# One level of Strassen's algorithm in the input projection of a fused decoder block

## The reference, cut to what matters

```
u = rms_norm(h, attn_pre_norm)                       # 1024 x 1024
c_q, c_kv, k_rope, m_q, m_k, m_v, m_o, m_i, m_f = split_cols(u @ w_in, IN_SIZES)
# widths       256   128   64      512  512  512  512  4    4
q  = rms_norm(c_q, q_norm) @ w_uq;   kv = rms_norm(c_kv, kv_norm) @ w_ukv
qk = silu(causal_dwconv(concat([m_q, m_k]), conv_w, conv_b))     # four taps along the sequence
hm = rms_norm(mlstm_chunkwise(mq, mk, m_v, m_i + bias_i, m_f + bias_f))
mlstm_out = sigmoid(m_o) * hm
```

## Time and profile before

| | |
|---|---|
| median of 3 runs | 1843.81 us |
| the profiled execution, from its first to its last instruction (span) | 1841.5 us |
| median less that span | 2.3 us |
| TensorE busy | 1815.9 us, 99% of the span |
| VectorE, ScalarE, GpSimd busy | 74%, 35%, 58% |

### The profile page before, as it was taken

The page is one execution under the profiler, slowest core; times in us unless marked ns, Lnnn a source line. Parts: engine busy times, 40 slices in busy tenths (PEclk is TensorE's granted clock), DMA queues, the critical chain, the costliest instruction groups (busy, mean ns, idle before and its releaser), DMA issues.

```text
span 1841.5 us, 22556 instructions
## 1 busy us (share of the span) xinstructions
PE 1815.9 (99%) x8610; PEld 1517.1 (82%) x8610; DVE 1360.6 (74%) x1530; ACT 640.1 (35%) x1140; POOL 1065.2 (58%) x749
## 2 busy tenths in 40 slices
PE   8999999999999999999999999999999999999998
PEld 8887889988887888888878888788788888888887
DVE  7777146666587666586589989667988885698897
ACT  5421157772331111111133433515433343333313
POOL 4443332260149988798877885632575455566564
PEclk9999999999999999999999999999999999999999
DMA  6121210033222333233366641112333232853232
GB/s 168 48 57 46 51 23 17 17 91 116 91 81 69 107 100 122 73 115 114 115 244 210 221 149 47 46 44 94 106 123 115 103 111 106 319 191 107 73 111 91
DMA packets 123322, 194.81 MB, mean 106 GB/s; under 512 B 31169, under 2 KB 87489, under 8 KB 120146
## 3 DMA queue, kind: packets, MB, share of 16 engines
q1 hardware_dynamic: 123184, 193.34, 31.2%
q10 hardware_dynamic: 34, 0.07, 0.0%
HBM read 144.56 MB, written 48.82 MB: 105 GB/s over the span
## 4 chain that ended last, share of the span: by engine, by line
PE 68%; DVE 5%; issue 2%; POOL 2%; ACT 1%; DMA 0%; DVEq 0%; SPq 0%; POOLq 0%
PE ps L1211 61%; PE ps L1517 1%; PE ps L1519 1%; PE ps L1518 1%; POOL ring_lo L1082 1%; POOL ring_hi L1081 1%; DVE y L3165 1%; PE ps L1764 1%; PE ps L1766 1%; PE ps L1765 1%; DVE y L3158 0%; PE ps L1642 0%; DVE xs_lo L2992 0%; DVE y L2883 0%; PE ps L1396 0%
## 5 line engine op out<-in xcount | busy, mean ns | idle before, releaser
L1211 PE MATMUL ps<-f_hi,ring_hi 128*128 128x512 f32 x384 | 149.7, 390 | 1.3 <-POOL ring_lo L1082 1.3
L1211 PE MATMUL ps<-f_hi,ring_lo 128*128 128x512 f32 x384 | 149.4, 389 | 0.0
L1211 PE MATMUL ps<-f_lo,ring_hi 128*128 128x512 f32 x384 | 149.4, 389 | 0.0
L972 POOL TENSOR_TENSOR w_lo<-stage,w_hi 128x1024 fp32r<-128x1024 f32 x48 | 125.7, 2618 | 4.0
L1145 POOL TENSOR_TENSOR ring_lo<-w_sum,ring_hi 128x512 fp32r<-128x512 f32 x60 | 95.3, 1600 | 50.2 <-ACT ring_hi L2215 50.1
L1211 PE MATMUL ps<-d_w_hi,d_hid_hi 128*128 128x512 f32 x312 | 121.5, 390 | 1.5 <-DVE hid L2858 1.1
L1082 POOL TENSOR_TENSOR ring_lo<-w_sum,ring_hi 128x512 fp32r<-128x512 f32 x80 | 118.4, 1480 | 6.7
L1211 PE MATMUL ps<-d_w_lo,d_hid_hi 128*128 128x512 f32 x312 | 121.4, 389 | 0.0
L1211 PE MATMUL ps<-d_w_hi,d_hid_lo 128*128 128x512 f32 x312 | 121.4, 389 | 0.0
L2115 ACT ACTIVATE f_copy<-ps 128x512 f32<-128x512 f32 x60 | 35.4, 597 | 226.2 <-PE ps L1211 207.3
L971 POOL TENSOR_SCALAR w_hi<-stage 128x1024 fp32r<-128x1024 f32 x48 | 61.5, 1281 | 73.6 <-PE ps L1211 61.5
(11 more groups left out here) (484 smaller groups left out, 5533.9 us busy)
## 6 DMA issues: line engine op xcount, KB each, us to landing
d_raw<-hid_rows SPq DMA_DIRECT2D x37, 512.0 KB, 4.5
stage<-in_w_up SPq DMA_DIRECT2D x22, 512.0 KB, 4.8
wd_raw<-in_w_down SPq DMA_DIRECT2D x22, 512.0 KB, 5.3
raw_w<-in_w_gate SPq DMA_DIRECT2D x20, 512.0 KB, 4.8
stage<-in_w_in SPq DMA_DIRECT2D x18, 512.0 KB, 3.7
stage<-in_pool_w_in SPq DMA_DIRECT2D x16, 512.0 KB, 5.1
raw_w<-in_pool_w_in SPq DMA_DIRECT2D x16, 512.0 KB, 4.8
m_rows<-u_row SPq DMA_DIRECT2D x16, 512.0 KB, 2.7
```

The costliest lines, as they stand in the source:

```text
L972: g.tensor_tensor(lo, stage[:, h, :], hi.bitcast(F32), ALU.subtract).then_inc(parted[h], 1)
L1211: last = mm(out_ap, l, r, start=(start and j == 0), stop=(stop and j == n - 1), skip_group_check=onto)
```

## The change

Tiles 2 to 7 of the projection (m_q, m_k, m_o) become six quads of seven products.

- The quarters of u are combined into four sums. POOL adds high and low parts of u back together (`u_rows`, 16 instructions), DVE forms 16 sums (`u_sums`), ACT takes their high parts (`u_sum_hi`) and DVE their low parts (`u_sum_lo`, 4 instructions of 2048 elements). The fourth sum is written over a quarter of u.
- V's rows are computed first, right behind tiles 0 and 1, with the four matmuls on the squares after their first 48 matmuls. V's rows and the latents are written to DRAM and read back, since their place in SBUF is used in between.
- For each quad SP loads two halves of weights, DVE forms four sums of them (`iq_sums`), ACT takes the high parts of the seven blocks (`iq_block_hi`) and POOL the low parts, PE multiplies, ACT copies three products (`iq_copy_product`) and DVE adds up. The convolutions of a quad's two row blocks stand in the middle of the sums of the quad after it.
- The head's weights, V's rows and the latents are fetched at the end of the last quad. Counts of semaphores that later stages share are shifted by constants, and the rest of the program is as it was.

The diff, cut to its core. In it `IN_QUADS` is 6, `IN_BLOCKS` 42, `V_TILE` 2, `TB` 8, and `US_ORDER` (1, 0, 2, 3):

```diff
+            sp.wait_ge(in_full, 12)
+            iq_load(0)
+            for h in range(2):
+                sp.wait_ge(parted[h], V_TILE + 2)
+            iq_load(1)
+            for t in range(TB):
+                sp.wait_ge(in_taken, 12 + t + 1)
+                sp.dma_start(v_dram[t], v_spill[t % 3][:]).then_inc(rows_in[t], 16)
+            sp.wait_ge(latent_ready, 1)
+            sp.wait_ge(act_head, 1)
+            sp.dma_start(lat_dram, lat[:].rearrange("p c t -> p (c t)")).then_inc(lat_spilled, 16)
...
+            for q in range(2, IN_QUADS):
+                sp.wait_ge(w_split, 7 * (q - 1))
+                iq_load(q)
...
+            sp.wait_ge(w_split, IN_BLOCKS)
+            sp.dma_start(c_kv[:], lat_dram[:, 2 * S:3 * S]).then_inc(lat_in, 16)
+            sp.dma_start(k_pe[:], lat_dram[:, 3 * S:4 * S]).then_inc(lat_in, 16)
+            sp.wait_ge(prod_full, IN_BLOCKS - 4)
             head_weights(0)
...
+            sp.wait_ge(prod_full, IN_BLOCKS - 3)
+            for t in range(TB):
...
+            sp.dma_start(m_v[:], v_dram.rearrange("t p n -> p t n")).then_inc(v_in, 16)
...
+            def u_rows(k):
+                if k == 0:
...
+                if k == 2:
+                    pool.wait_ge(early_dve, 1)
+                if k == 3:
+                    pool.wait_ge(fs_raw, 4)
+                for i, (half_k, n) in enumerate(((0, 1), (0, 0), (1, 1), (1, 0))):
+                    x_h, x_l = u_part(half_k, n)
+                    g.tensor_tensor(u_whole[k % 3][:, i, :], x_h[:, k, :].bitcast(F32), x_l[:, k, :].bitcast(F32),
+                                    ALU.add).then_inc(kpe_split, 1)
+
+            u_rows(0)
...
+            pool.wait_ge(in_full, 4)
+            part(V_TILE, 0, landed(V_TILE))
+            u_rows(2)
+            pool.wait_ge(in_full, 8)
+            part(V_TILE + 1, 1, landed(V_TILE + 1))
+            u_rows(3)
...
+            for q in range(IN_QUADS):
+                for o in range(7):
...
+                    pool.wait_ge(w_hi_ready, 7 * q + o + 1)
+                    g.tensor_tensor(as_blocks(lo, src), src, as_blocks(hi, src).bitcast(F32), ALU.subtract).then_inc(w_split, 1)
...
             in_tile(1, 1, 4, 4, first=True)
-            with pe.Fori(1, 3, 1) as i:
-                in_tile(2 * i, 0, 8 * i, 0)
-                in_tile(2 * i + 1, 1, 8 * i + 4, 4)
...
-            pe.wait_ge(sq_ready, 2)
...
-            in_tile(6, 0, 28, 4)
-            in_tile(7, 1, 32, 0)
-            value_rows(0)
-            value_rows(1)
+            value_rows(0, range(4))
+            pe.wait_ge(sq_ready, 2)
+            for j in range(4):
+                mm(ps[:, j, :], ones[:], sq[:, j // 2, (j % 2) * HALF:(j % 2 + 1) * HALF],
+                   start=True, stop=True).then_inc(in_full, 1)
+            value_rows(1, range(4))
+            value_rows(0, range(4, TB))
+            value_rows(1, range(4, TB))
...
+            for q in range(IN_QUADS):
+                if q < 2:
+                    pe.wait_ge(in_taken, 16 + 4 * q)
+                else:
+                    pe.wait_ge(c11_ready, q - 1)
+                    pe.wait_ge(quad_summed, 4 * (q - 1))
+                for o in range(7):
+                    pe.wait_ge(w_split, 7 * q + o + 1)
+                    if q == 0 and o in (1, 2, 3, 6):
+                        pe.wait_ge(fs_split, (1, 2, 3, 6).index(o) + 1)
...
+                if o in SUM_AT:
+                    act.wait_ge(w_summed, 4 * q + SUM_AT[o])
+                if q:
+                    act.wait_ge(prod_full, 7 * (q - 1) + o + 1)
+                elif o in (0, 4):
+                    act.wait_ge(in_full, 17 if o == 0 else 21)
+                f(as_blocks(iq_ring[o][0], src), src, ACT.Copy).then_inc(w_hi_ready, 1)
...
+                u_sum_hi(i)
+            for o in range(4):
+                iq_block_hi(0, o)
+            for t in range(4, TB):
+                value_row(t)
+            u_sum_hi(3)
+            for o in range(4, 7):
+                iq_block_hi(0, o)
...
+            for q in range(IN_QUADS):
+                if q == 0:
+                    act.wait_ge(fs_split, 4)
+                else:
+                    act.wait_ge(quad_summed, 4 * q - 2)
+                iq_copy_product(q, 0)
+                iq_block_hi(q + 1, 0)
+                iq_block_hi(q + 1, 1)
+                if q == IN_QUADS - 1:
...
+                iq_copy_product(q, 1)
+                iq_block_hi(q + 1, 2)
+                iq_copy_product(q, 2)
+                iq_block_hi(q + 1, 3)
+                iq_block_hi(q + 1, 4)
+                act.wait_ge(prod_full, 7 * q + 5)
+                if q < IN_QUADS - 1:
+                    if q:
+                        act.wait_ge(conv_done, 2 * q)
+                    f(conv_row[0][:, half(0)], ps[:, iq_bank(q), :], ACT.Copy).then_inc(c11_ready, 1)
+                    iq_block_hi(q + 1, 5)
+                    iq_block_hi(q + 1, 6)
...
+            def u_sums(k):
...
+                dve.wait_ge(kpe_split, 4 * k + 4)
+                v.tensor_tensor(us_raw[0][:, k, :], x01, x00, ALU.subtract).then_inc(fs_raw, 1)
+                v.tensor_tensor(us_raw[2][:, k, :], x11, x01, ALU.subtract).then_inc(fs_raw, 1)
+                dve.wait_ge(fs_raw, 4 * k + 1)
+                v.tensor_tensor(us_raw[1][:, k, :], x11, us_raw[0][:, k, :], ALU.subtract).then_inc(fs_raw, 1)
+                dve.wait_ge(fs_raw, 4 * k + 3)
+                v.tensor_tensor(us_raw[3][:, k, :], x10, us_raw[1][:, k, :], ALU.subtract).then_inc(fs_raw, 1)
...
-                own.do(dve, v.tensor_tensor(sq[:, m, :], c_q[:, m, :], c_q[:, m, :], ALU.mult))
...
+                own.do(dve, v.tensor_tensor(sq[:, m, :], c_q_raw[:, m, :], c_q_raw[:, m, :], ALU.mult))
+            own.do(dve, v.tensor_tensor(sq[:, 0, :], sq[:, 0, :], sq[:, 1, :], ALU.add))
+            u_sums(0)
+            u_sums(1)
             dve.wait_ge(in_taken, 6)
-            v.tensor_tensor(sq[:, 1, :], c_kv[:], c_kv[:], ALU.mult).then_inc(sq_ready, 1)
+            v.tensor_tensor(sq[:, 1, :], c_kv_raw[:], c_kv_raw[:], ALU.mult).then_inc(sq_ready, 2)
 
             dve.wait_ge(in_taken, 8)
...
+            u_sums(2)
+            u_sums(3)
+
+            dve.wait_ge(in_taken, 10)
...
+
...
+                w00, w01, w10, w11 = (iq_raw_block(q, c, k) for c in range(2) for k in range(2))
...
+                v.tensor_tensor(s[0], w10, w11, ALU.add).then_inc(w_summed, 1)
...
+            def conv(c):
...
+                own.do(dve, v.tensor_scalar(o, rows[:], conv_w[:, c, CONV - 1:CONV], conv_b[:, c:c + 1], ALU.mult, ALU.add))
+                for late in range(1, CONV):
+                    j = CONV - 1 - late
+                    ins = v.scalar_tensor_tensor(o[:, late:S], rows[:, 0:S - late], conv_w[:, c, j:j + 1], o[:, late:S],
+                                                 ALU.mult, ALU.add)
...
+            iq_sums(0)
+            for j in range(4):
+                u_sum_lo(j)
+            for q in range(IN_QUADS):
+                b0 = iq_bank(q)
+                convs = 1 <= q <= 4
...
+                iq_sums(q + 1)
+                dve.wait_ge(prod_full, 7 * q + 2)
+                dve.wait_ge(prod_copied, 3 * q + 1)
...
+                v.tensor_tensor(iq_copy[:, 3, :], iq_copy[:, 0, :], ps[:, b0 + 1, :], ALU.add).then_inc(quad_summed, 1)
+                if convs:
+                    dve.wait_ge(c11_ready, q)
+                    conv(2 * q - 1)
+                dve.wait_ge(prod_copied, 3 * q + 3)
+                own.do(dve, v.tensor_tensor(iq_copy[:, 1, :], iq_copy[:, 1, :], iq_copy[:, 2, :], ALU.add))
...
+                v.tensor_tensor(dst[3], iq_copy[:, 3, :], iq_copy[:, 1, :], ALU.add).then_inc(quad_summed, 1)
+                if convs:
+                    conv(2 * q - 2)
+                    dve.wait_ge(conv_done, 2 * q)
+                if q == IN_QUADS - 1:
+                    latent_parts()
+                for j, b in enumerate((2, 1)):
+                    dve.wait_ge(prod_full, 7 * q + 6 + j)
+                    v.tensor_tensor(dst[b], iq_copy[:, 3, :], ps[:, b0 + 2 + j, :], ALU.add).then_inc(quad_summed, 1)
```

More of the change, by code:

```diff
@@ L1910, in act_program @@
                 f(sd[:, half(j % 2)], ps[:, j, :], ACT.Sqrt, bias=EPS, scale=1.0 / width).then_inc(in_taken, 1)
-            act.wait_ge(gates_spilled, 64)
-            act.wait_ge(latent_ready, 1)
-            for c in range(HEADS):
-                for n in range(2):
-                    q = 28 + 2 * c + n
-                    act.wait_ge(in_full, q + 1)
-                    f(mix[:, 4 + c, half(n)], ps[:, q % 8, :], ACT.Sigmoid).then_inc(in_taken, 1)
-            f(rot_swapped[PAIR_A, :], rot[PAIR_B, :], ACT.Copy)
@@ new lines, in iq_copy_product @@
+            def iq_copy_product(q, j):
+                o = (0, 2, 3)[j]
+                act.wait_ge(prod_full, 7 * q + o + 1)
+                f(iq_copy[:, j, :], ps[:, iq_bank(q) + o, :], ACT.Copy).then_inc(prod_copied, 1)
+            for t in range(4):
```

(46 more changed lines are left out.)

480 lines of the change are left out of this document (273 added, 207 removed).

## The result

The changed kernel takes 1858.77 us (median of 4 runs, 1857.93 to 1860.05), the kernel before 1844.31 on the same chip: the ratio is 1.0078, with a 95% interval of 1.0066 to 1.0090. It is slower by 14.5 us, where the prediction had 1858.0.

A forecast was written before the change was run, and what follows sets the result against it. PE was taken to wait for nobody before the change, DVE and POOL to hold each other up. -16.3 + 8.7 + 6.3 + 4.0 + 4.6 + 5.0 + 2.2 = +14.5, rounded to +14.2, gave 1858.0 us, range 1846 to 1868.

The forecast's parts named there:

- Step 1: PE's matmuls in the projection: six quads of 84 instead of tiles of 96, 72 fewer, -16.3 us.
- Step 2: PE's wait for the squares, which DVE ends late at 84.4 beside POOL's additions and weight parts: +8.7 us.
- Step 3: PE's wait in V's rows for banks that ACT's square roots must read first, behind the gate rows: +6.3 us.
- Step 4: First quad: PE waits for ACT's copies of products, held up by DVE's low parts and weight sums: +4.0 us.
- Step 5: Quads 1 to 4: DVE needs 21.8 us each against PE's 19.0, so a late copy stops PE: +4.6 us.
- Step 6: Start of the heads: weights requested late, behind the latents, then split by POOL beside DVE: +5.0 us.
- Step 7: PE's clock falls to its lower level after three long idle times, some losses taken back: +2.2 us.
- A: Rival: DVE isn't held up early, so steps 2, 3 and most of 4 fall away; 1840 us, chance 0.12.
- B: Rival: DVE and POOL block each other for whole instructions, a pair costing 1.97 instead of 1.70; 1868 us, chance 0.12.
- C: Rival: the lag of step 5 doesn't build up, DVE ending each quad within 19.0 us; 1849 us, chance 0.14.

The follow-up runs named there:

- e3: Changed kernel with the requests of the head's weights placed before those of two latents instead of behind them; 1861.0 us.
- e4: Changed kernel with the three later taps of each of the 8 convolutions on 8 columns instead of about 1022; 1849.7 us.
- e2: Changed kernel with POOL's 16 additions cut to 8 of 512 columns and DVE's sums of u reading the high parts instead; 1843.5 us.
- e7: Changed kernel with five reorderings of SP's, ACT's and DVE's work at the end of the projection, nothing else; 1848.8 us.
- e1: Changed kernel with the eight sums of u that stand before DVE's last square moved behind the gate rows; 1858.2 us.
- e6: Changed kernel with DVE's two reciprocals gone, ACT making the inverse roots by logarithm and exponential; 1856.3 us.

## Why the prediction was right, step by step

Its sign, size and places hold, and so does its mechanism: DVE and POOL hold each other up, and PE waits for what DVE ends late. The waits of steps 2 to 6 were forecast at 28.6 us and measured 21.3; the clock's loss, 7.6 us instead of 2.2, stands in their place for the most part. That 1858.0 came out within a microsecond of 1858.8 is partly luck: single waits were off by up to 2.5 us, and 1.1 us lie in the preparation, which the sum doesn't have.

- **Step 1**, -16.3: PE has 504 matmuls for the six quads (3 x 96 on quarters of u and 3 x 72 on its sums). A quad without a wait takes 19.0 us.
- **Step 2**, +8.7: measured 7.60. Squares were expected at 84.4 and came at 84.5, but PE ended tile 1 at 65.9 instead of 64.8. These 1.1 us lie in the preparation, which the change doesn't touch, and in e3 and e4, the same code up to there, the squares' matmuls begin at 83.2 and 83.5. Counted from the preparation's end, then, DVE was 1.1 us faster than the sum. Two of the sum's terms don't hold: the 2 us that POOL was to do before DVE began (the additions begin at 37.60, the angles at 37.44), and the 2.8 for rot, which the earlier trace rows doesn't show (it has 2.42 for one of three instructions, beside POOL). The price of a pair, 1.70, was the number that mattered; e2 confirms it from the other side.
- **Step 3**, +6.3: measured 3.80. The first root let PE go on at 105.0 (forecast 104.6). PE had come at 101.2 instead of 98.3, mostly because at the lower clock the squares' four matmuls took 5.2 us (84.57 to 89.75) and not 3.0. The wait and the clock's loss in front of it are 6.4 us together: step 7 says that this loss is taken back here, and so it is.
- **Step 4**, +4.0: measured 2.04. DVE ended u's low parts at 138.4, against 138.5 expected. V's rows ended at 128.5 instead of 126.4, so product 5 came after the first copy and the 1.8 fell away; the 2.2 of the copy behind the second weight sum are the 2.04.
- **Step 5**, +4.6: measured 3.95, as 1.24 in quad 4 and 2.71 in quad 5. DVE's second convolutions end at 171.2, 193.0, 215.0 and 237.0, 21.8 to 22.0 us apart, where the step had 171.5, 236.9 and 21.8, and ACT's copy ends at 241.1 as forecast. Of each 22 us DVE stands idle for some 1.4, until POOL has made the low part of a quad's sixth block; the step didn't have this. e4 shows that the waits hang on this lag; e7 shows that the lag alone doesn't make them.
- **Step 6**, +5.0: measured 3.94. The weights were asked for at 241.67 (forecast 241.7), their split began at 248.46 and took 6.7 us; PE was ready at 251.3 instead of 249.3. What the step left out is a second condition: it counted the latents only as work that slows POOL's split, and e3 shows that they can set the start themselves.
- **Step 7**, +2.2: the clock fell after four waits, not three, and took 2.6, 1.7, 1.6 and 1.7 us (squares and first matmuls behind them 16.5 us instead of 13.9; in the others 12 matmuls in 4.4 us instead of 2.7). Only the last stands, behind the heads' start, as 1.7 of the 2.2 us by which the offset grows from there (+13.0) to the end (+15.2); where the other 0.5 lies isn't shown; the others lie inside what the waits that follow would have been.

The sum by measured terms: -16.3 + 1.1 + 21.3 of waits + 7.6 of clock = 13.7, and some 0.2 us for each of six waits, since a matmul's record (0.39) covers that much of the idle time behind it: 14.9, against 15.2.

Of the rivals, A (DVE isn't held up early, 1840) didn't come; e2, which takes the holding up away, measured 1843.5. B (blocked for whole instructions, 1.97 a pair) would have put the squares 4.5 us later; angles and additions alternate at 1.70. The Trainium skill, "SBUF — State Buffer", section "Who interferes with whom", calls the shared port an exclusive lock, and the trace agrees in so far as one engine's instruction goes at a time; of each pair 0.27 us overlap. C (no lag in the quads) isn't what came: the lag is there in quads 4 and 5. Its sum takes off 1 us more than its words name.

What the prediction's reading lacked is that its waits are not terms of their own. It added six waits, each by the order in front of it. e1 shows that those on squares, roots and quad 0 are one shortage on DVE, which can be moved at no gain, and e6 that relief in one place can come back as idle time in the next.
